# Attention steps 17 to 19: the last key rotation ahead of tile 19's shift, the heads' root behind its exponentials, the dummy root left out, the third spread behind its turns

## What is computed

```python
def diff_attention(q1, q2, k1, k2, v, lam):
    p = probs(q1, k1f) - lam * probs(q2, k2f)      # softmax of causal scores
    o = einsum('bhqs,bshe->bqhe', p, vf)
...
o_d = rmsnorm(o_d, g_diff_sub) * (1.0 - lam_init)  # one root and one factor a head and token
q_a, k_a = apply_rope(q_a), apply_rope(k_a)        # rotation of queries and keys
o_a = dsa_attention(q_a, k_a, v_a, q_i, k_i, w_i)  # softmax over the kept keys
mix = concatenate([o_a, o_d]);  y = einsum('bsc,cd->bsd', mix, w_out)
```

## Time and profile before

| | |
|---|---|
| time before, median of 3 | 1140.14 us (1140.05 to 1140.18) |
| the profiled execution's own time | 1140.28 us |
| its span in the trace | 1138.1 us |
| granted TensorE clock over the span | 0.998 |
| busy: PE, DVE, ACT, POOL | 1122.3, 674.1, 363.6, 692.7 us |

### The profile page before, as it was taken

How to read it: one execution, slowest core, us unless ns; L and a number is a source line. 1 busy time by engine, 2 the same in 40 slices (tenths; PEclk the granted TensorE clock), 3 DMA queues, 4 the chain that set the end, 5 groups by cost and what they waited for, 6 DMA issues and landing times.

```text
span 1138.1 us, 16627 instructions
## 1 busy us (share of the span) xinstructions
PE 1122.3 (99%) x5879; PEld 934.5 (82%) x5879; DVE 674.1 (59%) x1274; ACT 363.6 (32%) x744; POOL 692.7 (61%) x451
## 2 busy tenths in 40 slices
PE   7999999999999999999999999999999999999997
PEld 5888788998889998888778776777899888888886
DVE  4999868851158853447789777847885000455022
ACT  5134365540016531120211347546654000221012
POOL 7869947486636686667466333225847666666662
PEclk9999999999999999999999999999999999999999
DMA  6322222243213343324432222112224322332711
GB/s 249 129 76 72 75 75 93 81 143 111 92 56 112 112 148 98 105 93 133 125 113 94 92 83 65 33 46 74 75 75 167 111 93 93 97 106 93 167 56 74
DMA packets 51412, 113.35 MB, mean 100 GB/s; under 512 B 21520, under 2 KB 22160, under 8 KB 51344
## 3 DMA queue, kind: packets, MB, share of 16 engines
q1 hardware_dynamic: 31200, 105.40, 28.0%
q10 hardware_dynamic: 20144, 7.05, 2.7%
HBM read 102.99 MB, written 2.10 MB: 92 GB/s over the span
## 4 chain that ended last, share of the span: by engine, by line
PE 92%; DVE 5%; ACT 1%; issue 1%; DMA 0%; DVEq 0%; SPq 0%; ACTq 0%
PE bank L724 20%; PE bank L725 20%; PE bank L726 20%; PE bank L1331 5%; PE bank L1330 5%; PE bank L1332 5%; DVE bank L1953 3%; PE bank L1167 2%; PE bank L756 1%; PE bank L758 1%; PE bank L757 1%; PE bank L790 1%; PE bank L782 1%; PE bank L783 1%; PE bank L1181 1%
## 5 line engine op out<-in xcount | busy, mean ns | idle before, releaser
L538 POOL TENSOR_TENSOR wl<-raw,wh 128x1024 fp32r<-128x1024 f32 x156 | 376.1, 2411 | 13.0
L535 POOL TENSOR_SCALAR wh<-raw 128x1024 fp32r<-128x1024 f32 x156 | 167.1, 1071 | 306.0 <-PE bank L726 170.6
L724 PE MATMUL bank<-xh,wh 128*128 128x512 f32 (+2 forms) x712 | 260.4, 366 | 0.0
L726 PE MATMUL bank<-xh,wl 128*128 128x512 f32 (+2 forms) x712 | 255.3, 358 | 0.0
L725 PE MATMUL bank<-xl,wh 128*128 128x512 f32 (+2 forms) x712 | 255.0, 358 | 0.0
L724 PEld LDWEIGHTS bank<-xh,wh 128*128 128x128 f32 x712 | 134.1, 188 | 34.2 <-issue 16.2
L726 PEld LDWEIGHTS bank<-xh,wl 128*128 128x128 f32 x712 | 134.1, 188 | 19.6
L725 PEld LDWEIGHTS bank<-xl,wh 128*128 128x128 f32 x712 | 134.2, 188 | 17.8 <-issue 0.2
L724 PE MATMUL bank<-uh,wh 128*128 128x512 f32 x288 | 112.8, 392 | 0.0
L726 PE MATMUL bank<-uh,wl 128*128 128x512 f32 x288 | 112.1, 389 | 0.0
L725 PE MATMUL bank<-ul,wh 128*128 128x512 f32 x288 | 112.1, 389 | 0.0
(11 more groups left out here) (345 smaller groups left out, 2072.9 us busy)
## 6 DMA issues: line engine op xcount, KB each, us to landing
raw<-wstream SPq DMA_DIRECT2D x188, 512.0 KB, 3.5
x<-xT SPq DMA_DIRECT2D x8, 256.0 KB, 4.9
x4r<-x4b ACTq DMA_DIRECT2D x16, 128.0 KB, 3.4
out<-x4r SPq DMA_DIRECT2D x8, 256.0 KB, 2.0
qd<-ropey ACTq DMA_DIRECT2D x16, 64.0 KB, 2.1
kd<-ropey ACTq DMA_DIRECT2D x16, 64.0 KB, 2.1
qa<-ropey SPq DMA_DIRECT2D x16, 64.0 KB, 2.0
ka<-ropey SPq DMA_DIRECT2D x16, 64.0 KB, 2.0
```

What stands on the lines that cost most here:

```text
L535: nc.gpsimd.tensor_scalar(wh[c][:], raw[c][:], 1.0, 1.0, ALU.mult, ALU.mult).then_inc(high_ready, 1)
L538: nc.gpsimd.tensor_tensor(wl[c][:], raw[c][:], wh[c][:].bitcast(F32), ALU.subtract).then_inc(split_ready, 1)
L724: mm(out, wh_, mh, start=start, stop=False)
L726: return mm(out, wl_, mh, start=False, stop=stop)
```

## The change

Five things are moved or left out; nothing else of the program differs.

- DVE: `qk_second(9)` and `qk_join(9)` stood behind the shifts of steps 17 and 18. Now both stand in step 17, ahead of `shift(19)`.
- DVE: the reciprocal of the second two heads' roots stood in step 18 behind `shift(20)`; now it stands in step 19 ahead of `shift(21)`.
- ACT: `head_roots` of these heads stood in step 17 ahead of the exponentials of tile 19; now it stands behind them.
- ACT: a root of a constant at the end of step 16, whose result nothing reads, is gone.
- PE: spread 10 (head 2) stood in step 19 ahead of the piece and the turns of tile 19; now it stands behind them.

```diff
@@ PE step
-                if n in SPREAD_AT and SPREAD_AT[n] < 3:
+                if n in SPREAD_AT and SPREAD_AT[n] < 2:
...
                 if 0 <= n < TILES:
                     turn(n)
+                if n in SPREAD_AT and SPREAD_AT[n] == 2:
+                    pe.wait_ge(bc_used, 10)
+                    norm_spread(10)
@@ ACT step
-                if n == 17:
-                    head_roots(n)
...
-                if n == 16:
-                    A(soft[:, 31:32], eps[:, 0:1], ACT.Sqrt).then_inc(table_loaded, 1)
-                if n == 9:
+                if n in (9, 17):
                     head_roots(n)
@@ DVE step
+            def head_factors(b):
+
+                dve.wait_ge(sd_ready, 9 + b)
+                dve.wait_ge(bc_done, 8 + 2 * b)
+                V.reciprocal(rn[:, 0:8], sd[:, 0:8]).then_inc(rn_ready, 2)
...
+                if n == 17:
+                    qk_second(9)
+                    qk_join(9)
+                if n == 19:
+                    head_factors(1)
                 if n + 2 < TILES:
                     shift(n + 2)
-                if n in (12, 18):
-                    b = n // 18
-                    dve.wait_ge(sd_ready, 9 + b)
-                    dve.wait_ge(bc_done, 8 + 2 * b)
-                    V.reciprocal(rn[:, 0:8], sd[:, 0:8]).then_inc(rn_ready, 2)
+                if n == 12:
+                    head_factors(0)
...
-                if n in (2, 6, 10, 17):
-                    qk_second({2: 6, 6: 7, 10: 8, 17: 9}[n])
-                if n in (3, 7, 11, 18):
-                    qk_join({3: 6, 7: 7, 11: 8, 18: 9}[n])
+                if n in (2, 6, 10):
+                    qk_second({2: 6, 6: 7, 10: 8}[n])
+                if n in (3, 7, 11):
+                    qk_join({3: 6, 7: 7, 11: 8}[n])
```

## The result

| | before | changed |
|---|---|---|
| median | 1140.14 us (20 executions) | 1141.14 us (20 executions) |
| lowest to highest | 1139.58 to 1140.95 | 1140.16 to 1143.35 |
| the profiled execution | 1140.28, span 1138.1 | 1140.17, span 1138.0 |

The ratio is 1.0014, 95% interval 1.0007 to 1.002: 1.0 us slower in the median. It is within the 0.2% of "same" and within the range, but clear of noise and three times what was forecast. The spread has changed more than the median: the best executions of the changed kernel equal the old median, the worst lie 3.2 us above it. One of the 105 executions of the kernel before that are on record took 4217.6 us and is left out; the other 104 lie between 1139.48 and 1141.11.

What follows compares the result with a forecast made beforehand. PE was taken to bound the kernel (92% of the chain). The stall ahead of `turn(19)` goes but tile 18's delay eats it (+0.02); spread 11's wait makes it +0.31: 1140.14 + 0.3 = 1140.4 us, range 1139.4 to 1141.5.

Steps and rivals of the forecast that it cites:

- same: Outcome class for the whole kernel: time within 0.2% of the kernel before; chance 0.95.
- The hole and the joins: DVE ahead of `shift(19)`: POOL holds up both joins, so the shift starts at about 702.1 against 699.53, 2.57 later.
- DVE to PE: Tile 18: `normalise(18)` and `turn(18)` come 1.37 later; `turn(19)` starts at 706.53 without a wait, 0.18 earlier.
- What is late next: ACT's second table load delays head 2's low part to 710.83; spread 11 waits 0.29 and starts at 710.85: +0.31 us.
- (d): On ACT a stall d follows each table load, spread 11 at +0.31 + 2d; 1143.2 us with d 1.38; chance 0.02.
- It needs at most 0.93 more, is done by 704.26, and does not bind.: On PE, `scores(20)` waits for `shift(19)` until 703.33, yet finishes before `turn(18)` can go on at 704.46.
- (a): DVE's joins are hardly held, `shift(19)` starts at 700.2, spread 11 at 710.27 (-0.3): 1139.7 us; chance 0.25.
- (b): PE's waits ahead of `turn(18)` and `turn(19)` both go and nothing grows: -1.39, 1138.75 us; chance 0.08.
- (c): On DVE the second join also falls behind POOL's second L586 and ends at 703.8: +1.9, 1142.0 us; chance 0.08.

Runs made afterwards that it cites:

- e1: The changed kernel once more, unaltered: median 1141.54 us, ratio 1.0015 to the kernel before.
- e5: The changed kernel with one matmul of no use (512 columns) on PE ahead of `scores(20)`: median 1140.67 us, ratio 1.0008.
- e9: The changed kernel with two matmuls of no use (512 and 256 columns) on PE ahead of `scores(20)`: median 1140.63 us, ratio 1.0005.
- e4: The changed kernel with the two joins of key rotation 9 back in step 18, its products still ahead of `shift(19)`: median 1139.47 us, ratio 0.9994.
- e2: The kernel before with only the products and joins of key rotation 9 moved ahead of `shift(19)`: median 1142.85 us, ratio 1.0023.
- e3: The changed kernel with `qk_second(9)` and `qk_join(9)` back at their old places: median 1140.87 us, ratio 1.0005.
- e8: The kernel before with only key rotation 9 moved ahead of `shift(19)`, plus one 512-column matmul of no use ahead of `scores(20)`: median 1141.69 us, ratio 1.0014.
- e7: The changed kernel with key rotation 9 back and head 1's high part on ACT behind the exponentials of tile 19: median 1140.19 us, ratio 1.0001.

## Why the prediction was wrong, point by point

- **The hole and the joins: right.** `shift(19)` at 702.02 by the old count (701.39 + 0.63), forecast 702.1; each join 0.55 behind a POOL instruction. The rule of the Trainium skill on the shared pair ("SBUF — State Buffer", Who interferes with whom: the holder has it for its whole length, the other fully blocks) agrees: the first join ends behind L538 (699.79, 699.24), the second behind L586 (701.47, 700.93). The turn that DVE gets between two POOL instructions, taken from rows of before, is seen twice more.
- **DVE to PE: right.** The piece starts at 705.63 by the old count; the working gives 705.59 (706.53 less its 0.94). `turn(19)` waits for nothing.
- **What is late next: right in kind, 0.2 us short in size.** Low part of head 2 at 710.27 (forecast 710.14), spread 11 at 711.01 (710.85), its wait 0.36 (0.29). Net +0.52 at step 21 instead of +0.31. The table load takes 1.28 us and the root follows at once (703.66 + 1.28 = 704.94, the root at 704.95); nothing of rival (d) is to be seen.
- **The step that failed: "It needs at most 0.93 more, is done by 704.26, and does not bind."** This takes the wait of `scores(20)` at its length and puts what it does to the clock at nothing. The working's own numbers have 1.2 us of new idle time on PE (from 701.49 until the first half of `shift(19)` is out, 702.1 + 0.62 = 702.72); it gets no term, while the idle time ahead of `turn(19)` of about the same size (1.15) goes in exchange. But the two are not the same to the clock. In the profiled execution of the kernel before the clock stays at 1.00 behind its 1.15 us, and its 20 times keep within 1.4 us; behind the new 1.2 us it falls in part of the executions, for 6.8 us in e1, and that costs 2.4 us there. No rival named the granted clock. e5 and e9 show the cause by filling the gap alone (median +0.61), e4 by taking it away. So of the +1.00 measured some 0.5 is the chain of waits, forecast at 0.31, and the rest is this step.
- **Rivals (a), (b), (c), (d):** none happened. (c), a second collision with L586, did not come in the change, but a near relative of it did in e2, e3 and e8, with `normalise(18)` in the place of the join.

What stays open: why a gap ahead of `scores(20)` sets off the fall where one of equal length ahead of `turn(19)` did not (1.15 in the kernel before, 1.33 in e7). The two differ in what PE does around them (sums of single columns and short scores here, a full piece of the projection there), and no run separates that. The middle executions of the changed kernel (1140.7 to 1141.8, mean clock mostly 0.997 and 0.998), in which both its medians lie, were never caught in a profile. That they hold a short fall like the 3.4 us of e3 is argued, not shown; that they mostly go when the gap is filled is shown (e9).

## What to carry to other kernels

Where PE bounds the kernel, price a new idle time of PE by where it falls as well as by its length, and look at the spread and the mean clock of several executions: a profile of one can show the good case only. Filling the gap with a matmul of no use, timed over several executions, tells if the idle time itself is what is paid for. The mean clock of an execution shows a long fall only; it also takes in the tail in which PE has nothing left to do. And before work is moved into a hole of DVE, lay POOL's instructions beside the hole: products that read PSUM went through unhindered (0.67 and 0.68 us beside L538), instructions that read and write SBUF alone took 2.3 to 3.6 times their length (a join 1.57 and 1.74 instead of 0.69, a product of `normalise(18)` 1.19 to 1.50 instead of 0.42).

## What the runs showed of the hardware that was not expected

- The granted clock fell from 1.00 to 0.50 in the midst of dense work (in e1 PE was busy for 11.80 of the 13 us from 690 to 703), behind one idle time of 1.20 us (e1: 703.0 to 709.8) or 0.99 us (e3: 704.06 to 707.46), in some executions of a program and not in others.
- One unaltered program spreads over 3 us, 1140.16 to 1143.35, and its 11 executions above 1142 are those with a mean clock of 0.996 or 0.995.
- The clock also falls at the end of the kernel before, some 2.5 us behind the last matmul (1134.4 against 1131.8), and that fall alone brings the mean over the span to 0.998.
- An early finish on ACT can cost: POOL's L586, released 1.6 us earlier by it, met DVE and made `normalise(18)`'s product 1.19 instead of 0.42 us (e3).
